# Attention of a two-layer trunk: mask by TensorE, softmax from PSUM, and the difference of two maps taken while P is turned

## The chip, the cores and the metric

The kernel runs on one core of a Trainium2 chip. The metric is the device time in microseconds (us); the median of three runs is given. The engines are TensorE (PE, and PEld for its weight loads), VectorE (DVE), ScalarE (ACT), GpSimd (POOL) and SyncE (SP), which issues the large DMAs.

## What is computed

256 tokens of width 1024 go through two layers. Layer 0 has two kinds of attention, 8 heads each: A (latent attention, query and key of 96) and B (a band with a bias by relative position, 64), then a dense SwiGLU. Layer 1 has differential attention C, 8 heads of two maps each (64), then a top-2-of-8 expert SwiGLU. All is in float32.

```python
def chunk_causal_softmax(scores, q0):          # CHUNK = 64, Q_BLOCK = 128
    mask = k_chunk[None, :] <= q_chunk[:, None]
    return softmax(where(mask, scores, -inf))
# A: for each block of 128 queries, keys up to the block's end
s = q @ k.T * scale;  p = chunk_causal_softmax(s, q0);  out = p @ v
# C: two maps m of each head
s = einsum('bhmqd,bhmkd->bhmqk', q, k) * scale
p = chunk_causal_softmax(s, q0)
a = p[:, :, 0] - lam * p[:, :, 1]
out = a @ v;  then rmsnorm(out, g_sub) * (1 - lam_init)
```

## The kernel before

Each engine has its own program, written by hand in order; semaphores join them. Weights come in units of 1 MB by SyncE's DMAs into seven buffers `raw`. ScalarE copies each unit to `w_hi` (rounded, L641 and L878), VectorE takes the rest to `w_lo` (L1027, L1430), and TensorE makes three products of each pair of blocks (L1672 to L1674). These two steps are the "split" of a unit, `split_to(n)` in both programs. A buffer is loaded again once VectorE has split its unit.

The change touches the two attention loops. Both work on units: one unit is one map, with 128 x 128 scores for the first block of queries and 128 x 256 for the second, side by side as 384 columns of one PSUM bank. Three banks (0, 1, 6) hold scores in turn.

- TensorE, layer 0 (i from 0 to 20): `scores(i)` (L1760; the products L1765 and L1766), from i = 3 `turn_p(i - 3)` (three transposes, L1779), `keep_busy(2)` (products that nobody reads, L1772), from i = 5 `weigh_values(i - 5)` (L1793 to L1795). Heads 0 to 7 are A, with 96 rows, 8 to 15 are B, with 64 rows, each in one half of the array's rows.
- TensorE, layer 1 (i from 0 to 12): the same with two units an iteration (first map on rows 0 to 63, second map on rows 64 to 127) and `keep_busy(3)`. Then `out_projection` turns y (L1807) half by half.
- VectorE, `scores` (L1128): scales a unit, adds the mask (or B's bias with the mask in it) and writes it from PSUM to SBUF (L1136), then takes the two negated maxima of each row (L1140, L1141). In layer 1 `difference(i)` runs two iterations behind: a reciprocal (L1385), a factor for each row (L1386), and p0 + factor * p1 over 384 columns in SBUF (L1390). `head_outputs` (L1302) scales the outputs, `output_norm` (L1411 to L1415) norms y. At i = 8 and 9 of layer 1 it splits units 1 and 2 of the output projection.
- ScalarE, `exponentials` (L692): two exponentials in place in SBUF with the row sums (L695, L697), then `turn_p` (L705): the turned P from PSUM to SBUF, three units behind.
- TensorE's `scores` waits until VectorE has read the bank's last unit (`scores_read`), and its `turn_p` waits for the exponential (layer 0) or for the difference (layer 1), and for the copy of the turned P of two heads before.
- GpSimd makes constants at the start (a select of 128 x 128 at L585) and issues a few small DMAs, the last (L2143) for a gain after the first unit of layer 1's output projection.

## Time and profile before

| | |
|---|---|
| median of 3 runs | 1478.47 us (1476.52 to 1480.3) |
| profiled execution | 1479.04 us, span 1476.9 us |
| busy, share of the span | PE 97%, PEld 80%, DVE 80%, ACT 65%, POOL 1% |
| chain that ended last | PE 83%, DVE 10%, ACT 3%, issue 3%, DMA 1% |
| granted PE clock | 0.991 on average |
| HBM read | 419.28 MB, 285 GB/s over the span |

A row of a timeline gives the start, the duration, engine, line, operation, output and inputs, how many instructions were merged into it, and in brackets how long the engine idled before it and what ended that. Products of TensorE overlap in their pipeline, so what one costs in a row of them is the distance from start to start. Layer 0's attention loop is at 77.5 to 118 us, layer 1's at 409.8 to 448 us, the experts from 493 us on.

### The profile page before, as it was taken

The numbers are of one execution on the slowest core, as the hardware profiler recorded it, in microseconds if no ns is written. First come the engines' busy times: TensorE is split into PE (matmuls) and PEld (weight loads), VectorE is DVE, ScalarE is ACT, GpSimd is POOL, SyncE is SP. The second block draws the span as 40 slices with busy tenths as digits, with TensorE's granted clock in tenths as the row PEclk, the third lists the DMA queues.
The fourth block names the chain that finished last, engine by engine and source line by source line (L and its number), as shares of the span: only waits on it lengthen the run. The fifth ranks groups of instructions, "written<-read, shape, count | busy, mean of one in ns | idle before, by whom it ended". The sixth has DMA issues, their size and how long they took to land.

```text
span 1476.9 us, 17986 instructions
## 1 busy us (share of the span) xinstructions
PE 1427.5 (97%) x6705; PEld 1177.5 (80%) x6705; DVE 1177.6 (80%) x1003; ACT 959.4 (65%) x835; POOL 8.4 (1%) x49
## 2 busy tenths in 40 slices
PE   7899999999979899999999999999999999999998
PEld 6778788887757788888888888878888888888886
DVE  5984545446895799899898899879888988888986
ACT  5574533344564677777777777767776776777774
POOL 2000000000000000000000000000000000000000
PEclk9999999999999899999999999999999999999999
DMA  8404755375403599999999999989999999999993
GB/s 276 155 30 154 245 183 187 115 233 173 171 27 103 189 388 364 367 368 376 335 353 379 370 347 376 377 294 366 376 365 358 372 375 309 373 377 355 369 377 113
DMA packets 181604, 421.56 MB, mean 285 GB/s; under 512 B 9240, under 2 KB 12364, under 8 KB 181516
## 3 DMA queue, kind: packets, MB, share of 16 engines
q1 hardware_dynamic: 178460, 418.56, 79.1%
q0 software_dynamic: 560, 1.59, 0.4%
q8 instruction: 58, 0.95, 0.3%
q10 hardware_dynamic: 2496, 0.23, 0.1%
q14 instruction: 30, 0.25, 0.0%
HBM read 419.28 MB, written 1.06 MB: 285 GB/s over the span
## 4 chain that ended last, share of the span: by engine, by line
PE 83%; DVE 10%; ACT 3%; issue 3%; DMA 1%; ACTq 0%; DVEq 0%
PE ps L1672 25%; PE ps L1674 25%; PE ps L1673 25%; DVE w_lo L1027 2%; PE ps L2037 2%; DVE w_lo L1430 2%; ACT w_hi L641 1%; PE ps L2003 1%; DVE h L1559 1%; DVE work L1136 1%; PE ps L1772 1%; ACT w_hi L878 1%; PE ps L1779 0%; PE ps L2015 0%; PE ps L2014 0%
## 5 line engine op out<-in xcount | busy, mean ns | idle before, releaser
L1430 DVE TENSOR_TENSOR w_lo<-raw,w_hi 128x2048 fp32r<-128x2048 f32 x336 | 768.1, 2289 | 107.9 <-ACT w_hi L878 107.2
L878 ACT ACTIVATE w_hi<-raw 128x2048 fp32r<-128x2048 f32 x336 | 644.8, 1919 | 244.7 <-PE ps L1674 244.6
L1672 PE MATMUL ps<-w_hi,xT_hi 128*128 128x512 f32 (+2 forms) x1312 | 515.6, 393 | 14.8 <-issue 4.1
L1674 PE MATMUL ps<-w_hi,xT_lo 128*128 128x512 f32 (+2 forms) x1312 | 508.5, 388 | 0.0
L1673 PE MATMUL ps<-w_lo,xT_hi 128*128 128x512 f32 (+2 forms) x1312 | 507.4, 387 | 0.0
L1672 PEld LDWEIGHTS ps<-w_hi,xT_hi 128*128 128x128 f32 x1312 | 247.3, 189 | 67.9 <-issue 8.8
L1674 PEld LDWEIGHTS ps<-w_hi,xT_lo 128*128 128x128 f32 x1312 | 247.1, 188 | 51.0
L1673 PEld LDWEIGHTS ps<-w_lo,xT_hi 128*128 128x128 f32 x1312 | 247.6, 189 | 47.3
L1672 PE MATMUL ps<-w_hi,hT_hi 128*128 128x512 f32 (+1 forms) x548 | 214.7, 392 | 2.4 <-DVE hT_lo L1041 2.4
L1027 DVE TENSOR_TENSOR w_lo<-raw,w_hi 128x2048 fp32r<-128x2048 f32 (+4 forms) x65 | 138.3, 2137 | 98.1 <-ACT w_hi L641 97.9
L1674 PE MATMUL ps<-w_hi,hT_lo 128*128 128x512 f32 (+1 forms) x548 | 213.0, 389 | 0.0
L1673 PE MATMUL ps<-w_lo,hT_hi 128*128 128x512 f32 (+1 forms) x548 | 212.9, 388 | 0.0
L641 ACT ACTIVATE w_hi<-raw 128x2048 fp32r<-128x2048 f32 (+4 forms) x65 | 115.6, 1791 | 126.2 <-PE ps L1674 126.2
L1672 PEld LDWEIGHTS ps<-w_hi,hT_hi 128*128 128x128 f32 (+1 forms) x548 | 102.9, 188 | 25.0 <-DVE hT_lo L1041 2.6
L1674 PEld LDWEIGHTS ps<-w_hi,hT_lo 128*128 128x128 f32 (+1 forms) x548 | 102.9, 188 | 21.5
L1673 PEld LDWEIGHTS ps<-w_lo,hT_hi 128*128 128x128 f32 (+1 forms) x548 | 102.9, 188 | 20.3
L905 ACT ACTIVATE hT_hi<-ps 128x512 fp32r<-128x512 f32 x56 | 33.2, 592 | 9.8 <-PE ps L2037 9.8
L1565 DVE TENSOR_TENSOR hT_lo<-ps,hT_hi 128x512 fp32r<-128x512 f32 x56 | 38.3, 683 | 1.3 <-ACT hT_hi L905 1.3
L1592 DVE TENSOR_TENSOR prod_e<-sil_e,ps 128x512 f32<-128x512 f32 x56 | 38.1, 680 | 0.0
L2037 PEld LDWEIGHTS ps<-ident,prod_e 128*128 128x128 f32 x224 | 27.1, 139 | 12.0 <-DVE h L1559 2.9
L2037 PE MATMUL ps<-ident,prod_e 128*128 128x128 f32 x224 | 33.8, 273 | 2.8 <-DVE h L1559 2.8
L930 ACT ACTIVATE sil_e<-ps 128x512 f32<-128x512 f32 x56 | 32.3, 577 | 0.0
(264 smaller groups left out, 717.0 us busy)
## 6 DMA issues: line engine op xcount, KB each, us to landing
raw<-in_od_ex_gate_dram SPq DMA_DIRECT2D x112, 1024.0 KB, 5.8
raw<-in_od_ex_up_dram SPq DMA_DIRECT2D x112, 1024.0 KB, 6.3
raw<-in_od_ex_down_dram SPq DMA_DIRECT2D x112, 1024.0 KB, 6.1
raw<-in_od_w_qkv_dram SPq DMA_DIRECT2D x12, 1024.0 KB, 5.2
raw<-in_ev_ff_gate_dram SPq DMA_DIRECT2D x10, 1024.0 KB, 5.2
raw<-in_ev_ff_up_dram SPq DMA_DIRECT2D x10, 1024.0 KB, 6.0
raw<-in_ev_ff_down_dram SPq DMA_DIRECT2D x10, 1024.0 KB, 5.0
raw<-in_ev_w_in_dram SPq DMA_DIRECT2D x5, 1024.0 KB, 8.8
```

Source lines behind the costliest of these rows:

```text
L641: ins = act.activation(w_hi[0:r, n % SPLIT, a:a + m], raw[0:r, raw_of(n), a:a + m], ACT.Copy)
L878: act.activation(w_hi[:, (DENSE + q) % SPLIT, :], raw[:, r, :], ACT.Copy).then_inc(hi_ready, 1)
L905: act.activation(hT_hi[:, :, side(m)], blocks(4 + m % 2), ACT.Copy).then_inc(hT_part, 1)
L930: act.activation(sil_e[:, j % 2, :], ps[:, 2 * (j % 2), :], ACT.Silu).then_inc(silu_done, 1)
L1027: ins = dve.tensor_tensor(w_lo[0:r, n % SPLIT, a:a + m], raw[0:r, raw_of(n), a:a + m], w_hi[0:r, n % SPLIT, a:a + m].bitcast(F32), ALU.sub ...
L1430: dve.tensor_tensor(w_lo[:, k, :], raw[:, raw_of(DENSE + q), :], w_hi[:, k, :].bitcast(F32), ALU.subtract).then_inc(lo_ready, 1)
L1565: dve.tensor_tensor(hT_lo[:, :, side(m)], blocks(4 + m % 2), hT_hi[:, :, side(m)].bitcast(F32), ALU.subtract).then_inc(hT_ready, 1)
L1592: dve.tensor_tensor(prod_e[:, j % 2, :], sil_e[:, j % 2, :], ps[:, 2 * (j % 2) + 1, :], ALU.mult).then_inc(prod_done, 1)
L1672: pe.matmul(out, x_hi, hi, start=start, stop=False)
L1673: pe.matmul(out, x_hi, lo, start=False, stop=False)
L1674: return pe.matmul(out, x_lo, hi, start=False, stop=stop)
L2037: ins = pe.transpose(ps[:, 4 + j % 2, n * P:(n + 1) * P], prod_e[:, j % 2, n * P:(n + 1) * P], ident[:, :])
```

## The change

- For units of A and C TensorE adds the mask: a third product, identity by the mask's 64 rightmost columns, over the right halves of both diagonal blocks (`scores`, argument `masked`). The factor d^-1/2 moves into the gain columns of the queries.
- VectorE then only takes maxima, from PSUM; ScalarE takes the exponentials from PSUM and writes SBUF. B is as before (`band_scores`). The score bank of a masked unit is free after its exponential.
- VectorE instead of ScalarE copies the turned P for A and C.
- In layer 1 VectorE computes the row factors only. GpSimd makes two diagonal matrices from them, and TensorE takes the difference as it turns: for each of three blocks p0^T I + p1^T diag(factor), six f32 products instead of three transposes (`turn_difference`).
- `keep_busy` is 2 instead of 3 in layer 1. VectorE splits unit 1 of the output projection at i = 4 of the loop, unit 2 after the first half of y.

The diff, without semaphore declarations and blank lines:

```diff
@@ -283,6 +283,8 @@
 pt1 = carve(work, C_MIX, 2, 384)
+diag = carve(work, 4 * C_MIX, 2 * TT, P)
@@ -689,12 +693,16 @@
-    def exponentials(u, unit, s, slot):
+    def exponentials(u, unit, s, slot, slot_head, biased):
         act.wait_ge(max_ready, unit + 1)
-        act.activation(s[:, slot, 0:P], s[:, slot, 0:P], ACT.Exp,
+        if slot_head is not None:
+            act.wait_ge(p_psum, slot_head + 1)
+        src = s[:, slot, :] if biased else ps[:, score_bank(unit % 16), :]
+        act.activation(s[:, slot, 0:P], src[:, 0:P], ACT.Exp,
                        bias=negmax[:, u, 0:1], accum_out=psum_l[:, u, 0:1])
-        act.activation(s[:, slot, P:384], s[:, slot, P:384], ACT.Exp,
+        act.activation(s[:, slot, P:384], src[:, P:384], ACT.Exp,
                        bias=negmax[:, u, 1:2], accum_out=psum_l[:, u, 1:2]).then_inc(exp_done, 1)
@@ -777,8 +785,8 @@
         if i < A_HEADS + B_HEADS:
-            exponentials(i, i, s0, i % S0)
-        if i >= TURN_LAG:
+            exponentials(i, i, s0, i % S0, i - S0 if S0 <= i < A_HEADS else None, i >= A_HEADS)
+        if i >= A_HEADS + TURN_LAG:
             turn_p(i - TURN_LAG, pt0)
@@ -855,13 +863,12 @@
             for m in range(2):
-                exponentials(2 * i + m, A_HEADS + B_HEADS + 2 * i + m, s1, (2 * i + m) % S1)
+                exponentials(2 * i + m, A_HEADS + B_HEADS + 2 * i + m, s1, (2 * i + m) % S1,
+                             16 + i - S1 // 2 if i >= S1 // 2 else None, False)
         if i == C_HEADS:
...
             square_outputs(0)
-        if i >= TURN_LAG:
-            turn_p(A_HEADS + B_HEADS + i - TURN_LAG, pt1)
     output_roots(0)
@@ -1094,6 +1101,9 @@
+        dve.tensor_scalar(gcol[:, G_AQ:G_AQ + 1], gcol[:, G_AQ:G_AQ + 1], A_QK ** -0.5, None, ALU.mult)
+        dve.tensor_scalar(gcol[:, G_CQ:G_CQ + 1], gcol[:, G_CQ:G_CQ + 1], C_DH ** -0.5, None, ALU.mult)
         dve.tensor_scalar(gcol[:, G_SUB:G_SUB + 1], gcol[:, G_SUB:G_SUB + 1], 1.0 - LAM_INIT, None,
@@ -1125,20 +1135,35 @@
-    def scores(u, unit, s, slot, factor, added, slot_head):
+    def maxima(u, src):
+        dve.tensor_reduce(negmax[:, u, 0:1], src[:, 0:P], AX.X, ALU.max, negate=True)
+        dve.tensor_reduce(negmax[:, u, 1:2], src[:, P:384], AX.X, ALU.max, negate=True).then_inc(max_ready, 1)
+    def scores(u, unit):
         dve.wait_ge(scores_psum, unit + 1)
-        if slot_head is not None:
-            dve.wait_ge(p_psum, slot_head + 1)
-        for a, n, rows in added:
-            ins = dve.scalar_tensor_tensor(out=s[:, slot, a:a + n], in0=ps[:, score_bank(unit % 16), a:a + n], scalar=factor,
+        maxima(u, ps[:, score_bank(unit % 16), :])
+    def band_scores(head):
+        u = A_HEADS + head
+        slot, row = u % S0, bias[:, head, :]
+        dve.wait_ge(scores_psum, u + 1)
+        dve.wait_ge(p_psum, u - S0 + 1)
+        for a, n, rows in ((0, P, row[:, P:T]), (P, T, row)):
+            ins = dve.scalar_tensor_tensor(out=s0[:, slot, a:a + n], in0=ps[:, score_bank(u), a:a + n], scalar=B_DH ** -0.5,
                                            in1=rows, op0=ALU.mult, op1=ALU.add)
         ins.then_inc(scores_read, 1)
-        dve.wait_ge(scores_read, unit + 1)
-        dve.tensor_reduce(negmax[:, u, 0:1], s[:, slot, 0:P], AX.X, ALU.max, negate=True)
-        dve.tensor_reduce(negmax[:, u, 1:2], s[:, slot, P:384], AX.X, ALU.max, negate=True).then_inc(max_ready, 1)
+        dve.wait_ge(scores_read, head + 1)
+        maxima(u, s0[:, slot, :])
+    def turn_p(head, pt):
+        dve.wait_ge(p_psum, head + 1)
+        if head >= 2:
+            dve.wait_ge(pv_done, head - 1)
+        dve.tensor_copy(pt[:, head % 2, :], ps[:, 2 + head % 2, 0:384]).then_inc(p_turned_vec, 1)
@@ -1309,11 +1334,11 @@
         if u < A_HEADS:
-            added, factor = [(0, 384, mask[:, :])], A_QK ** -0.5
+            scores(u, u)
         else:
-            row = bias[:, u - A_HEADS, :]
-            added, factor = [(0, P, row[:, P:T]), (P, T, row)], B_DH ** -0.5
-        scores(u, u, s0, u % S0, factor, added, u - S0 if u >= S0 else None)
+            band_scores(u - A_HEADS)
+        if TURN_LAG <= u < A_HEADS + TURN_LAG:
+            turn_p(u - TURN_LAG, pt0)
         if u in (10, 14):
@@ -1379,27 +1404,24 @@
-    def difference(i):
+    def difference_factors(i):
...
         link(dve.reciprocal(rinv[:, 2 * i:2 * i + 2, :], psum_l[:, 2 * i:2 * i + 2, :]))
-        link(dve.scalar_tensor_tensor(out=coef[:, i, :], in0=psum_l[:, 2 * i, :], scalar=lams[:, 5:6],
-                                      in1=rinv[:, 2 * i + 1, :], op0=ALU.mult, op1=ALU.mult))
-        a, b = (2 * i) % S1, (2 * i + 1) % S1
-        for t, (c0, c1) in enumerate(((0, P), (P, 384))):
-            ins = dve.scalar_tensor_tensor(out=s1[:, a, c0:c1], in0=s1[:, b, c0:c1], scalar=coef[:, i, t:t + 1],
-                                           in1=s1[:, a, c0:c1], op0=ALU.mult, op1=ALU.add)
-        ins.then_inc(diff_done, 1)
-    for i in range(C_HEADS + DIFF_LAG):
+        dve.scalar_tensor_tensor(out=coef[:, i, :], in0=psum_l[:, 2 * i, :], scalar=lams[:, 5:6],
+                                 in1=rinv[:, 2 * i + 1, :], op0=ALU.mult, op1=ALU.mult).then_inc(coef_ready, 1)
+    for i in range(C_HEADS + TURN_LAG):
         if i < C_HEADS:
             for m in range(2):
-                scores(2 * i + m, 16 + 2 * i + m, s1, (2 * i + m) % S1, C_DH ** -0.5, [(0, 384, mask[:, :])],
-                       16 + i - S1 // 2 if i >= S1 // 2 else None)
-        if i >= C_HEADS - 1:
-            split_to(AT["out1", 0, 0] + i - C_HEADS + 2)
-        if i >= DIFF_LAG:
-            difference(i - DIFF_LAG)
+                scores(2 * i + m, 16 + 2 * i + m)
+        if i == C_HEADS // 2:
+            split_to(AT["out1", 0, 0] + 2)
+        if DIFF_LAG <= i < C_HEADS + DIFF_LAG:
+            difference_factors(i - DIFF_LAG)
+        if i >= TURN_LAG:
+            turn_p(16 + i - TURN_LAG, pt1)
         if i in (7, 9):
@@ -1418,6 +1440,7 @@
     low_y(1, 0)
+    split_to(AT["out1", 0, 0] + 3)
     output_norm(1)
@@ -1757,24 +1780,57 @@
-    def scores(unit, q, k):
-        if unit % 16 >= len(SCORE_BANKS):
-            pe.wait_ge(scores_read, unit - len(SCORE_BANKS) + 1)
+    def scores(unit, q, k, masked):
+        last = unit - len(SCORE_BANKS)
+        if A_HEADS <= last < A_HEADS + B_HEADS and unit < 16:
+            pe.wait_ge(scores_read, last - A_HEADS + 1)
+        elif unit % 16 >= len(SCORE_BANKS):
+            pe.wait_ge(exp_done, last + 1)
         b = score_bank(unit % 16)
-        pe.matmul(ps[:, b, 0:P], q(0), k(P), start=True, stop=True)
-        pe.matmul(ps[:, b, P:384], q(1), k(T), start=True, stop=True).then_inc(scores_psum, 1)
+        pe.matmul(ps[:, b, 0:P], q(0), k(P), start=True, stop=not masked)
+        ins = pe.matmul(ps[:, b, P:384], q(1), k(T), start=not masked, stop=not masked)
+        if masked:
+            diagonal = ps[:, b, :].rearrange("p (t n) -> p t n", t=TT)[:, :, CHUNK:P]
+            ins = pe.matmul(diagonal, ident[:, :], mask[:, CHUNK:P].unsqueeze(1).to_broadcast([P, TT, CHUNK]),
+                            start=False, stop=True)
+        ins.then_inc(scores_psum, 1)
...
             pe.matmul(ps[:, 7, :], xT_hi[:, n, 0:P], xT_hi[:, 0:2, :].rearrange("p c n -> p (c n)"), start=True, stop=True)
+    def wait_turned(head):
+        if head < A_HEADS:
+            pe.wait_ge(p_turned_vec, head + 1)
+        elif head < A_HEADS + B_HEADS:
+            pe.wait_ge(p_turned, head - A_HEADS + 1)
+        else:
+            pe.wait_ge(p_turned_vec, head - B_HEADS + 1)
+    def turn_difference(n):
+        head, a, b = 16 + n, 2 * n % S1, (2 * n + 1) % S1
+        pe.wait_ge(diag_ready, n + 1)
+        wait_turned(head - 2)
+        for k in range(3):
+            cols_k = slice(k * P, (k + 1) * P)
+            bank = ps[:, 2 + head % 2, cols_k]
+            pe.matmul(bank, s1[:, a, cols_k], ident[:, :], start=True, stop=False)
+            ins = pe.matmul(bank, s1[:, b, cols_k], diag[:, TT * (n % 2) + min(k, 1), :], start=False, stop=True)
+        ins.then_inc(p_psum, 1)
...
         if head >= 2:
-            pe.wait_ge(p_turned, head - 1)
+            wait_turned(head - 2)
         for n in range(3):
@@ -1873,11 +1929,11 @@
         if i < A_HEADS:
-            scores(i, lambda t: qta[0:A_QK, i, t * P:(t + 1) * P], lambda n: kta[0:A_QK, i, 0:n])
+            scores(i, lambda t: qta[0:A_QK, i, t * P:(t + 1) * P], lambda n: kta[0:A_QK, i, 0:n], True)
         elif i < heads:
...
             r = slice(m * B_DH, (m + 1) * B_DH)
-            scores(i, lambda t: qtb[r, pair, t * P:(t + 1) * P], lambda n: ktb[r, pair, 0:n])
+            scores(i, lambda t: qtb[r, pair, t * P:(t + 1) * P], lambda n: ktb[r, pair, 0:n], False)
         if TURN_LAG <= i < heads + TURN_LAG:
@@ -1964,11 +2020,11 @@
                 r = slice(m * C_DH, (m + 1) * C_DH)
-                scores(16 + 2 * i + m, lambda t: qtc[r, i, t * P:(t + 1) * P], lambda n: ktc[r, i, 0:n])
+                scores(16 + 2 * i + m, lambda t: qtc[r, i, t * P:(t + 1) * P], lambda n: ktc[r, i, 0:n], True)
         if TURN_LAG <= i < C_HEADS + TURN_LAG:
             n = i - TURN_LAG
-            turn_p(16 + n, diff_done, n + 1, s1, 2 * n % S1)
-        keep_busy(3)
+            turn_difference(n)
+        keep_busy(2)
         if i >= VALUE_LAG:
@@ -2139,6 +2195,14 @@
+    for i in range(C_HEADS):
+        pool.wait_ge(coef_ready, i + 1)
+        if i >= 2:
+            pool.wait_ge(p_psum, 16 + i - 1)
+        for t in range(TT):
+            ins = pool.tensor_scalar(diag[:, TT * (i % 2) + t, :], ident[:, :], coef[:, i, t:t + 1], None, ALU.mult)
+        ins.then_inc(diag_ready, 1)
     pool.wait_ge(unit_used, AT["out1", 0, 0] + 1)
```

## Rows read from the trace of the kernel before

**Rows 1.** Busy time by stretches: each engine's busy us (instructions), PEclk, DMA share, GB/s.

```profile
77.50:130.00 52.50, 49.80 (x307) 41.92 (x308) 32.52 (x73) 31.87 (x90) 0.00 (x0) 1.00 0.07 21
...
409.50:448.00 38.50, 29.80 (x175) 21.81 (x175) 34.29 (x89) 22.79 (x77) 0.00 (x0) 0.91 0.18 55
```

**Rows 2.** Costliest groups of the page: busy us, mean ns, idle before, releaser.

```profile
L878 ACT ACTIVATE w_hi<-raw 128x2048 fp32r<-128x2048 f32 x336 | 644.8, 1919 | 244.7 <-PE ps L1674 244.6
```

**Rows 3.** Timeline of TensorE, heads of A in layer 0: start, us, [idle before <-releaser].

```profile
82.74 0.39 PE L1765 MATMUL ps<-raw 96*128 96x128 f32 x2
...
84.19 0.38 PE L1765 MATMUL ps<-raw 96*128 96x128 f32 x2
...
87.94 0.52 PE L1779 MATMUL ps<-ident,work 128*128 128x128 f32 x3 [0.74 <-ACT work L705]
```

**Rows 4.** Timeline of TensorE, one head of B in layer 0.

```profile
94.00 0.49 PE L1765 MATMUL ps<-raw 64*128 64x128 f32 x2
...
94.85 0.55 PE L1779 MATMUL ps<-ident,work 128*128 128x128 f32 x3
95.15 0.70 PE L1772 MATMUL ps<-xT_hi 128*128 128x512 f32 x2
95.70 0.33 PE L1793 MATMUL ps<-work 128*128 128x64 f32 x2
...
96.09 0.39 PE L1795 MATMUL ps<-work 128*128 128x64 f32 x2
96.40 0.48 PE L1765 MATMUL ps<-raw 64*128 64x128 f32 x2
```

**Rows 5.** Timeline of TensorE, first pair of layer 1.

```profile
409.79 0.50 PE L1765 MATMUL ps<-work 64*128 64x128 f32 x4 [0.94 <-DVE work L1126]
...
410.65 0.96 PE L1772 MATMUL ps<-xT_hi 128*128 128x512 f32 x3
```

**Rows 6.** Timeline of VectorE, layer 1's loop and its end.

```profile
429.16 0.55 DVE L1136 SCALAR_TENSOR_TENSOR work<-ps,mask 128x384 f32<-128x384 f32 x1
...
431.85 0.75 DVE L1390 SCALAR_TENSOR_TENSOR work<-work,coef 128x128 f32<-128x128 f32 x2
...
432.51 0.55 DVE L1136 SCALAR_TENSOR_TENSOR work<-ps,mask 128x384 f32<-128x384 f32 x1
...
436.46 2.28 DVE L1027 TENSOR_TENSOR w_lo<-raw,w_hi 128x2048 fp32r<-128x2048 f32 x1
...
444.92 1.22 DVE L1411 TENSOR_REDUCE ss<-work 128x8 f32<-128x1024 f32 x1 [1.12 <-ACT work L849]
```

**Rows 7.** Timeline of TensorE, layer 1's loop and its end.

```profile
429.30 0.55 PE L1779 MATMUL ps<-ident,work 128*128 128x128 f32 x3 [0.57 <-DVE work L1390]
...
430.39 0.39 PE L1793 MATMUL ps<-work 128*128 128x128 f32 x2
430.61 0.39 PE L1794 MATMUL ps<-work 128*128 128x128 f32 x2
...
439.93 0.55 PE L1779 MATMUL ps<-ident,work 128*128 128x128 f32 x3 [2.01 <-DVE work L1390]
...
448.03 1.09 PE L1807 MATMUL ps<-ident,xs 128*128 128x128 f32 x8
```

**Rows 8.** Timeline of TensorE, first products of the two output projections.

```profile
119.95 0.47 PE L1672 MATMUL ps<-w_hi,xT_hi 128*128 128x512 f32 x1 [1.62 <-issue]
...
450.95 0.47 PE L1672 MATMUL ps<-w_hi,xT_hi 128*128 128x512 f32 x1 [1.83 <-issue]
...
451.96 0.39 PE L1673 MATMUL ps<-w_lo,xT_hi 128*128 128x512 f32 x1
```

**Rows 9.** Groups of instructions of GpSimd.

```profile
L585 POOL TENSOR_SCALAR_AFFINE_SELECT ident<-ident 128x128 f32<-128x128 f32 x1 | 0.3, 282 | 0.2 <-POOL mask L583 0.2
```

**Rows 10.** Busy time by stretches, the two with the lower clock.

```profile
418.00:425.00 7.00, 6.34 (x24) 4.19 (x26) 6.25 (x20) 4.03 (x17) 0.00 (x0) 0.51 0.00 0
452.00:456.00 4.00, 4.00 (x12) 3.16 (x11) 1.61 (x3) 0.30 (x1) 0.00 (x0) 0.57 0.02 4
```

More of the change, by code:

```diff
@@ L364, in trunk @@
         exp_done = sem("exp_done")
-        diff_done = sem("diff_done")
+        coef_ready = sem("coef_ready")
+        diag_ready = sem("diag_ready")
         p_psum = sem("p_psum")
         p_turned = sem("p_turned")
+        p_turned_vec = sem("p_turned_vec")
         pv_done = sem("pv_done")
@@ L1786, in weigh_values @@
                 per = 2 if layer else 4
-                pe.wait_ge(p_turned, head + 1)
+                wait_turned(head)
                 if n % per == 0 and n >= 2 * per:
```

## The prediction

> **What bounds the kernel now.** I read the views in this order: the busy time by stretches, the timeline of TensorE (PE) and VectorE (DVE) through the two attention loops, then the clock.
>
> The stretches [rows 1] hold the two loops that the change touches. In layer 0 PE is busy 49.80 of 52.50 us at full clock: PE bounds it. In layer 1 PE is busy 29.80 of 38.50 us and DVE 34.29 of 38.50: DVE bounds it. Outside, the expert phase waits for PE alone (ScalarE's wait for a free buffer, 244.6 us in total, ends with a product [rows 2]), and its DMAs start as buffers come free, so what is won or lost in the loops passes to the end one to one.
>
> In layer 0 the timeline shows PE back to back. A head of A without values takes 84.19 - 82.74 = 1.45 us; the one stall of note is 0.74 us, for a turned P that ScalarE owes [rows 3]. A head of B takes 96.40 - 94.00 = 2.40 us: 0.85 for its scores (94.00 to 94.85), 0.30 for three transposes, 0.55 for two filler products, 0.39 up to the last value product and 0.31 from there to the next head [rows 4].
>
> In layer 1 one iteration scores a pair, two maps of 64 rows each. Where nothing holds PE, the pair takes 410.65 - 409.79 = 0.86 us [rows 5]. Two heads of 64 rows thus cost what one costs in layer 0 (0.85 [rows 4]): the two halves of the array work side by side. DVE needs 432.51 - 429.16 = 3.35 us for an iteration [rows 6], and PE idles for it: 0.57 us in the middle, 2.01 us near the end [rows 7], where two splits of 2.28 us stand in DVE's queue [rows 6]. From the first score (409.79) to the first transpose of y (448.03) it is 38.24 us [rows 5, 7].
>
> **DVE and ScalarE, part by part.** Each masked unit loses its scaled addition (0.55 us [rows 6]); the maxima stay, read from PSUM. The difference loses its two long operations (0.75 us [rows 6]) and keeps the two short ones. DVE gains the copy of P out of PSUM, 384 columns, which I take at 0.55 us, what the addition over 384 columns from PSUM takes now. An iteration of layer 1: 3.35 - 2 x 0.55 - 0.75 + 0.55 = about 2.0 us. ScalarE loses the copy. Neither is late any more, if PE's iteration gets longer than that. The two extra scalings of a gain column lie early beside products; I charge 0.1 us for them in all.
>
> **PE, layer 0.** Each of the 8 masked heads gains a product of 128x128 weights on 128 columns of f32. Its price: the start-to-start distance of two such products, 0.22 us (430.39 to 430.61 [rows 7]). 8 x 0.22 = 1.8 us. The stall of 0.74 us should go, as DVE now makes that copy and has no split before it. The banks now wait for the exponential of unit i - 3, not its reading; the turn that follows on PE waits for the same exponential anyway, so this costs little. With 0.2 us lost on that, layer 0 gets 1.2 us longer less some start-up slack: + 1.0 (bounds 0 and + 2.5, the latter if the three splits on ScalarE and DVE each show for 0.3 us and the stall stays).
>
> **PE, layer 1: the term that decides.** The mask is a product over all 128 rows, and it now stands between the scores of the first map and those of the second. They can't run side by side any more: each costs what a lone 64-row head costs in layer 0. So for one iteration:
> - scores 2 x 0.85, two masks 2 x 0.22, and 0.09 for the way back to 64 rows between them (0.31 less 0.22 [rows 4]): 2.23 us, for 0.86 before;
> - the turn: six f32 products with fresh weights, 6 x 0.22 = 1.33 us, for three transposes at 0.30;
> - fillers: two, 0.55, for three;
> - values unchanged: 0.22 + 0.22 + 0.31 = 0.75, or 0.67 where no scores follow.
>
> The loop has 3 iterations of scores and fillers (2.87 with the 0.09 back), 2 with the turn (4.20), 3 with values too (4.86), 3 with turn and values (2.55) and 2 with values (1.22): 8.6 + 8.4 + 14.6 + 7.6 + 2.4 = 41.6 us. DVE (2.0 us) and ScalarE (four exponentials, under 2 us) are far below 4.86. At the end of the loop y's first norm (3.11 us from its reduction on DVE at 444.92 to the transposes at 448.03 [rows 6, 7]) starts one copy after the last turn, while PE has 3.66 us of work after it (0.55 + 0.67 + 2 x 1.22): the two end within 0.2 us of each other, as now. So the loop goes from 38.24 to about 41.7 us: + 3.4 (bounds below, with the rivals: - 3.3 and + 6.4). Here the rule of the Trainium skill that speaks against the change is in "TensorEngine Tiling (Array Packing)", Key Properties: tiles work in parallel, but changing the tiling mode drains the engine. The trace agrees, 0.86 us for a pair against 0.85 for one. Without that rule, the pair still side by side, the sum would be that of the second rival below.
>
> **GpSimd.** It makes two diagonals of 128x128 an iteration. The nearest row is a 128x128 select at 0.28 us [rows 9]. From the last score of iteration 2 (409.8 + 7.9) DVE takes some 1.2 us for maxima and factors, so the diagonals may start at 419.0; PE wants them at 409.8 + 8.6 + 2.2 = 420.6. Up to 1.6 us for the pair is hidden at the tightest place, later over 3 us; I charge nothing (bounds 0, and 1 us if one takes four times the select). Its later DMA of a gain waits for a much later event. No DMA of the weight stream waits for GpSimd.
>
> **The moved splits.** Weight unit 1 of the output projection is split at iteration 4 on DVE, beside 4.2 us of PE; unit 2 after the first half of y. This delays the second norm by 2.2 us: now it would be ready some 3.0 us after the projection's first product, then 5.3. PE reaches the place after 24 products, four of which take 451.96 - 450.95 = 1.01 us at full clock [rows 8], so 5.5 to 6 us: just hidden (bounds 0 and 0.5). SyncE may load unit 2's buffer again only after its split, some 10 us later than now; the experts, who use it, start at 493 us, so I charge nothing.
>
> **The clock.** PE's granted clock is near 0.5 (the lower level, 1.2 GHz; 0.51 on average from 418 to 425 us, 0.57 from 452 to 456, where a part is at full speed) [rows 10], the second time after 1.83 us of idle PE [rows 8]. The first costs little now as DVE sets the pace. The second hits the projection: 4 us at 0.57 lose 1.7 us of full-speed work. In layer 0 the same end of loop, with 1.62 us idle [rows 8], has no fall. After the change the loop is dense, but the 1.83 us idle before the projection stays [rows 8]. I take half: - 0.9 (bounds 0 and - 1.7).
>
> **Sum.** 0.1 (gain columns) + 1.0 (layer 0) + 3.4 (layer 1) + 0 (GpSimd, splits) - 0.9 (clock) = + 3.6 us. The profiled execution took 1479.04 us (a span of 1476.9 and 2.1 around it), so it becomes 1482.6; the median of the three runs is 1478.47, 0.6 below the profiled one, and from it the change comes out at 1482.1 us.
>
> **The rivals.**
> - *PE keeps more overlap than I give it.* If each map costs what a head of A does, 0.60 us (1.45 less 0.30 and 0.55 [rows 3, 4]), instead of 0.85, the loop is 16 x 0.25 = 4.0 us shorter: 1478.1, no change. Against it stands each head of B in layer 0.
> - *The pair still runs side by side, mask and all.* Then scores cost 0.86 + 0.44 + 0.09 an iteration and the loop is 8 x 0.84 = 6.7 us shorter: 1475.4, faster than before, by DVE's relief. For it: nothing but that two of the three products are still of 64 rows.
> - *Slower: the lower clock comes into layer 1's loop.* PE now sets the pace there, so that a fall as at 418 us (6 us long) costs 3 us, which it doesn't today; and the fall at the projection stays, 0.9. It decides once PE idles some 2 us before the first turn, that is, if the first diagonals come 2 us late. 1486.0.
> - *The change doesn't relieve anything*: only if maxima and exponentials from PSUM were far slower than from SBUF. The 384-column addition that reads PSUM today takes 0.55 us in all [rows 6]; nothing speaks for it, and up to 4.86 us an iteration it wouldn't be seen.
>
> **Numbers.** Forecast 0.47 (own range 1479.5 to 1485), no-premium 0.15, side by side 0.12, lower clock or other stalls 0.26. 0.3% is 4.4 us, about what a measurement of this kernel tells from no change. Slower by more: a good third of the forecast's chance (above 1482.9) and nine tenths of the last, 0.40. Faster by more (below 1474.0): a third of the side-by-side case and a little: 0.06. The rest, 0.54, is within. The range 1475 to 1487.5 leaves out 2 in 10, by the loop's bounds on the one side and the stalls on the other.
>
> **What would show it.** In layer 1's loop PE busy without gaps, an iteration of scores, turn and values near 4.9 us, DVE busy for 2 us of it; the second map's first score block 0.3 us or more behind the first mask; turn products 0.22 us apart. In layer 0 the first 8 heads 0.22 us longer. Wrong, if PE waits for GpSimd, if an iteration comes out at 4 us, or if the clock in the loop is below 1.

## The result, and the profile after

The changed kernel takes 1484.97 us in the median of 20 runs (1481.88 to 1496.64), the kernel before 1478.10 (1476.43 to 1480.93), so it is 6.9 us slower by the medians (a quotient of 1.0046). The ratio on record is 1.0067, 95% interval [1.0052, 1.0082]; it is that of the means, 1488.11 and 1478.21, and so 9.9 us. The forecast was 1482.1 us, 3.6 us slower.

The 20 runs fall into two groups, and the mean granted clock of TensorE tells them apart: 13 runs at 1481.9 to 1485.9 us with a clock of 0.993 to 0.995, and 7 at 1493.5 to 1496.6 with 0.984 to 0.986. (The expectation of the first experiment below says 14 and 6, a miscount.) The kernel before has no second group. The first group is 5.8 us over before (1483.94), and the means lie further apart than the medians because of the second. The profiled execution is of the first: 1483.94 us, a span of 1482.1, which is 4.9 us more than the profiled execution of before.

| from - to | before | after | forecast |
|---|---|---|---|
| layer 0, first score to first transpose of y | 77.84 - 117.29: 39.45 | 77.90 - 118.33: 40.43 | + 1.0 |
| layer 1, the same | 409.79 - 448.03: 38.24 | 411.15 - 456.16: 45.01 | + 3.4 |
| first product of layer 1's output projection | 450.95 | 459.08 | |
| first gather of the experts | 486.91 | 493.91 | |

So layer 0 came out as forecast, and layer 1's loop got 6.8 us longer instead of 3.4. Busy time by stretches (from and to, length, then the busy us of PE, PEld, DVE, ACT, POOL, then PEclk, DMA share, GB/s), to be set beside [rows 1] and, for the last, [rows 10]:

```profile
410.00:415.00 5.00, 4.06 (x21) 2.40 (x19) 2.12 (x6) 3.27 (x9) 0.00 (x0) 1.00 0.00 0
415.00:420.00 5.00, 5.00 (x25) 3.16 (x24) 2.11 (x8) 3.01 (x14) 0.00 (x0) 1.00 0.00 0
...
435.00:440.00 5.00, 5.00 (x33) 4.02 (x32) 2.10 (x7) 1.82 (x8) 1.18 (x2) 1.00 0.00 0
...
460.00:465.00 5.00, 5.00 (x17) 3.95 (x17) 3.74 (x4) 0.30 (x1) 0.00 (x0) 0.71 0.54 166
```

PE is full and DVE at 2.1 of 5 us, where DVE stood at 34.29 of 38.50 [rows 1]: the bound moved to PE. One iteration with scores, turn and values on PE's timeline (start us, us; a row of x2 is one f32 product):

```profile
434.26 0.48 PE L1793 MATMUL ps<-work 64*128 64x128 f32 x2
434.59 0.59 PE L1794 MATMUL ps<-work 64*128 64x256 f32 x2
435.11 0.49 PE L1798 MATMUL ps<-mask,ident 128*128 128x128 f32 x2
435.53 0.48 PE L1793 MATMUL ps<-work 64*128 64x128 f32 x2
435.86 0.59 PE L1794 MATMUL ps<-work 64*128 64x256 f32 x2
436.38 0.49 PE L1798 MATMUL ps<-mask,ident 128*128 128x128 f32 x2
436.70 0.39 PE L1826 MATMUL ps<-ident,work 128*128 128x128 f32 x2
436.93 0.39 PE L1827 MATMUL ps<-work 128*128 128x128 f32 x2
...
437.96 0.71 PE L1806 MATMUL ps<-xT_hi 128*128 128x512 f32 x2
438.51 0.38 PE L1849 MATMUL ps<-work 128*128 128x128 f32 x2
...
439.27 0.49 PE L1793 MATMUL ps<-work 64*128 64x128 f32 x2
```

The two maps stand one behind the other (L1798 is the mask); the pair of [rows 5], where both lay in one row of x4 and took 0.86 us, is gone. The iteration takes 439.27 - 434.26 = 5.01 us. From a map's mask to the next map's score it is 0.42 us (435.11 to 435.53), from the second mask to the turn 0.32 (436.38 to 436.70), where two products of 128 rows stand 0.22 to 0.23 apart.

The idle times of PE in the loop and behind it:

```profile
447.28 0.49 PE L1826 MATMUL ps<-ident,work 128*128 128x128 f32 x2 [0.34 <-POOL work L2203]
456.16 1.09 PE L1863 MATMUL ps<-ident,xs 128*128 128x128 f32 x8 [1.41 <-DVE xs L1437]
459.08 0.47 PE L1695 MATMUL ps<-w_hi,xT_hi 128*128 128x512 f32 x1 [1.83 <-issue]
```

One more wait for GpSimd, of 0.19 us, stands at 431.60. A wait costs more than the idle time in brackets, since the products behind it start late as well. By the starts, the first of these turns comes 0.36 us late (0.68 us after its mask for 0.32) and loses 0.09 more inside; the second comes 0.50 us late (0.73 us after the last value product, 0.23 at 449.85). Together they cost 0.95 us. GpSimd's diagonals, by its groups of instructions:

```profile
L2203 POOL TENSOR_SCALAR work<-ident,coef 128x128 f32<-128x128 f32 x16 | 9.5, 602 | 414.5 <-DVE coef L1412 414.5
```

And DVE at the loop's end, where the 1.41 us come from:

```profile
450.12 0.56 DVE L1166 COPY work<-ps 128x384 f32<-128x384 f32 x1 [2.17 <-PE ps L1851]
450.59 0.68 DVE L1327 TENSOR_TENSOR xs<-ps,rinv 128x512 f32<-128x512 f32 x1
452.59 0.56 DVE L1166 COPY work<-ps 128x384 f32<-128x384 f32 x1 [1.32 <-PE ps L1851]
453.06 1.21 DVE L1433 TENSOR_REDUCE ss<-work 128x8 f32<-128x1024 f32 x1
454.64 0.20 DVE L1435 RECIPROCAL rs<-rs 128x8 f32<-128x8 f32 x1 [0.37 <-ACT rs L861]
454.88 1.22 DVE L1437 TENSOR_TENSOR xs<-xs,rs 128x1024 f32<-128x1024 f32 x1
```

DVE is idle 2.17 and 1.32 us in front of its last two copies. Each copy waits for the values of the head two before (L1851), which must have read the buffer of pt1 that the copy overwrites, and the norm of the first half of y (L1433 to L1437) is queued behind the copies. It ends at 456.10; PE has had no work since 454.75.

### The profile page after: what moved, and what is told of

Its sections match the earlier page's. It is cut to its first block, busy times and chain, and to the rows that moved or that the text cites. A ratio compares the mean times of both kernels' runs of the same rounds, so it can differ in the third digit from the quotient of the medians.

```text
span 1482.1 us, 18184 instructions
## 1 busy us (share of the span) xinstructions
PE 1441.3 (97%) x6812; PEld 1190.4 (80%) x6812; DVE 1168.0 (79%) x981; ACT 951.3 (64%) x819; POOL 17.9 (1%) x65
## 4 chain that ended last, share of the span: by engine, by line
PE 84%; DVE 9%; ACT 3%; issue 3%; DMA 1%; POOL 0%; ACTq 0%; DVEq 0%; POOLq 0%
PE ps L1695 25%; PE ps L1697 25%; PE ps L1696 25%; DVE w_lo L1034 2%; PE ps L2093 2%; DVE w_lo L1453 1%; PE ps L2059 1%; ACT w_hi L645 1%; DVE h L1582 1%; PE ps L1806 1%; PE ps L1794 1%; PE ps L1793 1%; ACT w_hi L885 1%; PE ps L1798 0%; PE ps L2071 0%
## 5 line engine op out<-in xcount | busy, mean ns | idle before, releaser
L1615 DVE TENSOR_TENSOR prod_e<-sil_e,ps 128x512 f32<-128x512 f32 x56 | 38.1, 680 | 0.0
```

The source lines that it names most:

```text
L1615: dve.tensor_tensor(prod_e[:, j % 2, :], sil_e[:, j % 2, :], ps[:, 2 * (j % 2) + 1, :], ALU.mult).then_inc(prod_done, 1)
```

## The experiments

All comparisons are against the kernel before, run beside them (medians 1477.36, 1477.88 and 1478.62 us for the three sets of runs). The ratio need not be the quotient of the medians; it lies above it where some runs are of the second group. "Loop" is layer 1's, from the first score to the first transpose of y, in the profiled execution.

| kernel | us (median) | ratio, interval | loop us | runs with a clock of 0.987 or less |
|---|---|---|---|---|
| as changed | 1484.53 | 1.0052 [1.0033, 1.007] | 45.01 | 9 of 28 |
| masks_after_pair | 1481.28 | 1.0023 [1.0014, 1.0031] | 42.83 | 0 of 11 |
| copy_on_scalar | 1480.34 | 1.0028 [1.0011, 1.0045] | 43.05 | 1 of 11 |
| no_fillers_l1 | 1481.51 | 1.0041 [1.0024, 1.0058] | 40.91 | 3 of 12 |
| turn_one_map | 1478.92 | 1.001 [1.0, 1.002] | 39.35 | 1 of 11 |
| fillers_before_loop | 1483.92 | 1.0041 [1.0028, 1.0055] | 45.02 | 0 of 5 |
| the same again | 1484.64 | 1.0047 [1.0035, 1.006] | 45.02 | 0 of 6 |
| pair_and_copy | 1477.33 | 0.9997 [0.9986, 1.0007] | 38.25 | 0 of 11 |
| layer0_alone | 1476.94 | 0.9996 [0.9987, 1.0005] | 37.64 | 0 of 11 |
| pair_copy_one_filler | 1479.24 | 1.0009 [0.9998, 1.0019] | 36.90 | 0 of 12 |
| pair_copy_no_filler | 1477.80 | 0.9998 [0.999, 1.0007] | 38.96 | 0 of 12 |
| one_filler_both_layers | 1472.26 | 0.9957 [0.9944, 0.997] | 36.90 | 0 of 5 |

(The first row has the time of the experiment, the loop of the first profile and the runs of both. The medians take in the runs with the low clock. Without them they are 1483.94 us as changed, 1480.2 for copy_on_scalar, 1481.05 for no_fillers_l1 and 1478.8 for turn_one_map. The low run of turn_one_map is further off than the others, 1500.89 us at a clock of 0.977; it was not profiled. Of the kernel before, none of 101 runs is more than 3.3 us above the median of its set; one, of 1481.12 us, has a clock of 0.987.)

### The changed kernel once more: the second group of times

> The changed kernel itself, nothing left out. 6 of its 20 runs took 1493 to 1497 us at a mean granted clock near 0.985, the other 14 took 1482 to 1486 at 0.993 to 0.995. Theory C (the clock falls in layer 1's attention loop, where TensorE now sets the pace, and stays low over much of it): about 3 runs in 10 lie 10 to 13 us above the rest with a clock near 0.985. Rival (the fall lies in another stretch, which the kernel before has too): the kernel before shows such runs as often in the same rounds.

Two of its 8 runs were at 1494.7 and 1495.0 us with a clock of 0.985, and the profiled execution (a span of 1493.2) is one of them. So this trace shows what the second group is. PE at the loop's head:

```profile
412.40 0.46 PE L1793 MATMUL ps<-work 64*128 64x128 f32 x2 [0.94 <-DVE work L1136]
412.69 0.59 PE L1794 MATMUL ps<-work 64*128 64x256 f32 x2
...
416.06 0.79 PE L1793 MATMUL ps<-work 64*128 64x128 f32 x2
416.65 1.06 PE L1794 MATMUL ps<-work 64*128 64x256 f32 x2
...
421.51 0.79 PE L1793 MATMUL ps<-work 64*128 64x128 f32 x2
```

and by stretches:

```profile
415.00:420.00 5.00, 5.00 (x15) 2.82 (x13) 1.25 (x4) 2.10 (x10) 0.00 (x0) 0.50 0.00 0
...
430.00:435.00 5.00, 5.00 (x20) 3.70 (x18) 1.48 (x5) 1.82 (x8) 1.18 (x2) 0.50 0.00 0
435.00:440.00 5.00, 5.00 (x31) 3.69 (x30) 3.00 (x5) 1.83 (x8) 0.00 (x0) 1.00 0.00 0
```

The clock falls to its lower level (0.50, 1.2 GHz) at 414.5 us and stays there for 20 us, though PE is busy all the time. An iteration of scores and fillers takes 421.51 - 416.06 = 5.45 us; in the first profile it takes 3.00. Twenty us of full PE at half clock are 10 us of work lost, and the medians of the groups lie 11.2 us apart. In the two profiles (spans of 1482.1 and 1493.2) 9.3 of 11.1 us are in the loop, 54.28 for 45.01; another 1.25 us were lost ahead of it, with a clock of 0.98 for 1.00 from 118 to 200 us. Before, the same stretch has its fall too [rows 10], but DVE sets the pace there and it costs little (0.6 us, by layer0_alone below).

### Both scores, then both masks

```diff
 # layer 1, TensorE
 for m in range(2):
     scores(16 + 2 * i + m, ..., True)     # without its mask product
+for m in range(2):
+    add_mask(16 + 2 * i + m)              # the mask product, then scores_psum
```

> In layer 1 the scores of both maps are issued first, the two mask products after them. Nothing is left out. Theory A (the mask between the two maps ends their running side by side and adds two switches of the array's row mode an iteration): the pair costs 0.9 us again, an iteration of scores, turn and values falls from 5.0 to about 3.8 us, and the kernel is 8 x 1.2 = 9 to 10 us faster than the changed one, near 1475. Rival B (the number of products sets the loop, not their order): no change, 1484 to 1485.

Measured: 1481.28 us, 3.2 less than the changed kernel (2.7 less than its first group) where 9 to 10 were expected, and the loop 2.2 us shorter. The pair is in one row again:

```profile
435.11 0.50 PE L1793 MATMUL ps<-work 64*128 64x128 f32 x4
435.43 0.61 PE L1794 MATMUL ps<-work 64*128 64x256 f32 x4
435.97 0.71 PE L1807 MATMUL ps<-mask,ident 128*128 128x128 f32 x4
436.52 0.39 PE L1834 MATMUL ps<-ident,work 128*128 128x128 f32 x2
...
439.08 0.50 PE L1793 MATMUL ps<-work 64*128 64x128 f32 x4
```

The pair takes 435.97 - 435.11 = 0.86 us, the very figure of [rows 5], and the iteration 439.08 - 435.11 = 3.97 us instead of 5.01. So one product of 128 rows between two 64-row maps is enough to end their running side by side. A wait for a bank isn't what did it: in iteration 0 all banks are free, and there too the maps start 1.24 us apart as changed and together here. The loop didn't get 8 x 1.04 us shorter, since other waits came up. In iterations 1 to 3 the second map starts 1.04 us behind the first, and the iterations take 3.00, 3.00 and 4.33 us as before this edit. By the program its bank is free only after the exponential of three units before; the idle time that ScalarE ends there shows in pair_copy_one_filler. And one turn waits long for GpSimd:

```profile
430.82 0.77 PE L1834 MATMUL ps<-ident,work 128*128 128x128 f32 x2 [1.53 <-POOL work L2213]
```

The factors of that head stand on DVE behind the split of iteration 4, 2.28 us long. The clock fell in that place too (0.66 from 430 to 435 us). This iteration takes 7.39 us (427.72 to 435.11) for 5.46 as changed, so it gives back 1.9 of the 4 us that the whole pairs gain. The 1.41 us at the loop's end stayed.

### The turned P copied by ScalarE again

```diff
-# VectorE, layer 1:   if i >= TURN_LAG: turn_p(16 + i - TURN_LAG, pt1)
+# ScalarE, layer 1:   if i >= TURN_LAG: turn_p(A_HEADS + B_HEADS + i - TURN_LAG, pt1)
```

> In layer 1 ScalarE copies the turned P again, as before the change; all else as changed. Theory D (TensorE's 1.41 us of idle at the loop's end and its short waits for GpSimd come from VectorE, which stands in its copy until the values of two heads before are done, with the factors and the norm queued behind): the idle goes, the loop ends 1.5 to 2 us earlier, 1482.5 to 1483.5 us. Rival (the norm's chain is late whoever copies): no change.

Measured: 1480.34 us, 4.2 less than the changed kernel (3.7 between the first groups); the loop 43.05 us. In front of the transposes of y the idle time is gone, for DVE gets to its reduction early:

```profile
448.39 0.69 DVE L1329 TENSOR_TENSOR xs<-ps,rinv 128x512 f32<-128x512 f32 x1 [2.66 <-PE ps L1851]
450.20 1.22 DVE L1433 TENSOR_REDUCE ss<-work 128x8 f32<-128x1024 f32 x1 [1.12 <-ACT work L857]
...
454.33 1.23 DVE L1437 TENSOR_TENSOR xs<-xs,rs 128x1024 f32<-128x1024 f32 x1
```

It now reduces at 450.20, before the last two copies are due, and the scaling ends at 455.56, when PE's own work ends too (455.55). The queue behind the copies on VectorE was the cause of the 1.41 us. But the copies hold up the norm on ScalarE as well. Its root of the sum of squares (L861) stands behind the last copy, and DVE waits 2.68 us for it:

```profile
453.39 0.49 ACT L713 ACTIVATE work<-ps 128x384 f32<-128x384 f32 x1 [1.98 <-PE ps L1851]
453.77 0.29 ACT L861 ACTIVATE rs<-ss,eps 128x8 f32<-128x8 f32 x1
454.10 0.20 DVE L1435 RECIPROCAL rs<-rs 128x8 f32<-128x8 f32 x1 [2.68 <-ACT rs L861]
```

Only the root, the reciprocal and the scaling are left behind the last copy there, where on VectorE the reduction stands behind it too, and what is left just hides under PE's own work. The loop is 2.0 us shorter, 1.3 from there and 0.5 from the second wait for GpSimd, which went as well. The median gives 2 us more than the loop; the traces don't show from where (the profiled execution, 1484.05 us, is itself the slowest of the ten without the low clock). The one run at 1493.72 us is of the second group.

### No fillers in layer 1's loop

```diff
-                keep_busy(2)        # layer 1
+                keep_busy(0)
```

> The changed kernel without any filler product in layer 1's loop. Theory E (TensorE sets the pace, the fillers cost their full time and the clock holds without them): 13 x 0.5 us = 6 us faster, near 1479, clock as before. Rival C (the fillers hold the clock up in a loop of short f32 products): more of the runs, or all, lie 10 us higher or more, with a clock of 0.985 or below.

Measured: 1481.51 us and a loop of 40.91, 4.1 less, with PE idle for 2.02 us at its end. The two fillers are worth 0.46 to 0.50 us an iteration by the starts (three iterations of scores took 2.50, 2.54 and 2.53 us for 3.00), 6 us in all. Two thirds of that came through; the rest went into longer waits, of PE for GpSimd (0.65, 0.32 and 0.34 us) and at the end. So PE sets the pace of most of the loop but not of all of it, and theory E's 6 us were too many. 3 of 12 runs were at 1490.1 to 1491.5 us with a clock of 0.987: the second group needs no fillers, and the fillers don't keep it off.

### The turn of one map alone

```diff
-pe.matmul(bank, s1[:, a, cols_k], ident[:, :], start=True, stop=False)
-ins = pe.matmul(bank, s1[:, b, cols_k], diag[...], start=False, stop=True)
+ins = pe.transpose(bank, s1[:, a, cols_k], ident[:, :])
```

> The changed kernel, layer 1 turning only the first map's P by three transposes; the second map and its diagonals are left out of the turn (they are still made). Theory (layer 1's loop is bound by TensorE, so each product counts): 24 products of 0.22 us go, 5.3 us, and the waits for GpSimd, 0.5 us: 1484.5 - 5.8 = 1478.7 us. Rival (the loop is bound by the chain of copies and values, pt's two buffers): under 2 us gained, 1482.5 us or more.

Measured: 1478.92 us, 5.6 less than the changed kernel; the loop 39.35, 5.7 less. That is what was expected, 5.8, but the agreement is luck. The edit also puts a transpose in place of each first product, and a transpose costs less:

```profile
436.07 0.49 PE L1826 MATMUL ps<-ident,work 128*128 128x128 f32 x3
436.31 0.71 PE L1806 MATMUL ps<-xT_hi 128*128 128x512 f32 x2
```

Three transposes take 0.24 us here (436.07 to 436.31) where the six products take 1.26 (436.70 to 437.96 in the first profile). An iteration without a wait is 1.02 us shorter (3.99 for 5.01), 8 us over eight heads and not 5.3. Some 2.5 us of that go back into waits for GpSimd, since PE comes earlier (1.20, 0.87, 0.38 and 0.28 us idle), and the end still has its 1.42. What the experiment shows is that the loop is bound by PE's products, against the rival's 2 us. The turn's price in the forecast is shown by the rows of the changed kernel, 0.22 us from one product to the next.

### Fillers in the idle time ahead of the loop

```diff
+for n in range(5): pe.matmul(ps[:, 4, :], xT_hi[:, n, 0:P], ...)   # 128x512, unread
 pe.wait_ge(qk_normed, 3)
 ...
+for n in range(3): pe.matmul(ps[:, 4, :], xT_hi[:, n, 0:P], ...)
 pe.wait_ge(proj_vec[1], QKV_J)
```

> The changed kernel with 5 and 3 unread products of 128x512 in TensorE's two idle times before layer 1's loop (1.43 and 0.94 us). Theory (the clock falls at the head of the loop in some runs because of the idle time before it): no run with a mean clock near 0.985 and 10 us more; the others as the changed kernel, 1483.8 us. Rival (the fall comes from the loop's own short products): about 3 in 10 runs are at 1493 to 1497 us as before.

> The same kernel as fillers_before_loop, for more executions of it: five were too few to tell a share of 3 in 10 from none. Theory (the idle time before the loop lets the clock fall): again no run with a mean clock near 0.985, all at 1483 to 1486 us. Rival (the loop's own short products do it): about 3 in 10 at 1493 to 1497 us.

(Two waits for the bank, in front of the five, are left out of this cut.) PE's idle times of 1.45 and 0.94 us became 0.31 and 0.24. All 11 runs have a clock of 0.992 to 0.995 and 1483.2 to 1487.2 us; the rest of the loop is as it was, 45.02 us. With a share of 9 in 28 for the changed kernel, eleven in a row without one happen by chance (19/28)^11 = 1.4 times in 100. So the idle time ahead of the loop very likely has a part in it. It isn't all. Four kernels have their masks behind both maps and that same idle time (masks_after_pair, pair_and_copy, pair_copy_one_filler, pair_copy_no_filler), and 0 of their 46 runs have a mean clock of 0.987 or less; four have the mask between the maps and the idle time (as changed, copy_on_scalar, no_fillers_l1, turn_one_map), with 14 of 62. So the runs speak for both together as what the 20 us fall needs. That it is the pairs isn't shown: in iterations 1 to 3, where the long fall runs, the maps stand apart with the masks behind them too, and one of these four, pair_copy_no_filler, has a fall of 10 us in just that place (below), short enough for its mean clock to stay at 0.991. How the chip weighs all this stays open.

### The edits together, and layer 0 by itself

pair_and_copy joins the first two edits and moves the split away from the factors:

```diff
-                if i == C_HEADS // 2:
+                if i == 9:
                     split_to(AT["out1", 0, 0] + 2)
```

> The changed kernel with three edits to layer 1 at once: both maps' scores before both masks, the turned P copied by ScalarE again, and VectorE's split of a weight moved from iteration 4 (where the factors of a head stood behind it) to iteration 9. Theory (the loss is made of separate terms: broken pairs, copies that wait ahead of the norm, factors that wait behind the split): the gains of the first two add up, 1484.5 - 3.2 - 4.2 = 1477.1 us, and the waits of TensorE for GpSimd and for the norm at the loop's end are gone; the loop lasts 42.8 - 1.5 - 1.4 = 39.9 us. Rival (one cover for the other: what one edit frees, the next wait takes): no better than the better of the two, 1480.3 us.

Measured: 1477.33 us, ratio 0.9997. That is 0.2 us from the 1477.1 worked out, and the loop is 38.25 us, that of before. No idle time stands at its end; two waits for GpSimd are left, 0.16 and 0.22 us. The agreement in the time doesn't prove the sum, for it had no term for the split and the loop is 1.65 us shorter than the 39.9 expected. The split's place is the reason: iteration 5 takes 3.97 us (428.03 to 432.00) for the 7.39 in masks_after_pair, 3.4 us less, of which the expectation counted the idle 1.5 and not the clock's fall behind it. With that 42.83 - 3.4 - 1.3 = 38.1 us, near the 38.25. So each of the three edits has its term in the loop.

layer0_alone gives layer 1 its code of before (the scaling of C's gain column goes as well) and keeps layer 0 as changed.

> The changed kernel with layer 1 as it was before (mask and difference on VectorE, three fillers, copies by ScalarE, splits where they were); layer 0 and the gain columns as changed. Theory (layer 0's masks cost 1.0 us on TensorE and nothing comes back): 1477.4 + 1.0 = 1478.4 us, the loop of layer 1 38.2 us long again, no run with a mean clock near 0.985. Rival (layer 0's later end shifts what follows, and the rest of the loss is there): over 1480 us.

Measured: 1476.94 us, ratio 0.9996 [0.9987, 1.0005], so the 1.0 us of layer 0 can't be told from nothing in the time. In its trace it is there: 79.07 to 119.50 is 40.43 us, as in each kernel with this layer 0 and two fillers, against 39.45 before. Layer 1's loop was 37.64 us, 0.6 shorter than before, as the clock didn't fall in it (1.00 from 410 to 450 us). None of its 11 runs has a clock of 0.991 or less; of the 27 runs of before beside them 11 have. Among runs at 0.993 and above the medians are 1476.9 and 1476.6. Why the old loop keeps its clock behind the new layer 0 isn't settled.

Then fewer fillers, on top of pair_and_copy.

```diff
-                keep_busy(2)        # layer 1
+                keep_busy(1)        # pair_copy_one_filler; (0): pair_copy_no_filler
-                keep_busy(2)        # layer 0
+                keep_busy(1)        # one_filler_both_layers, with (1) in layer 1
```

> pair_and_copy with one unread product of 128x512 instead of two in each iteration of layer 1's loop. Theory (TensorE sets the pace of that loop): 13 products of 0.27 us less, 3.5 us, but the last five iterations wait for the copies (0.5 us): the loop 38.25 - 3 = 35.2 us, the time 1477.3 - 3 = 1474.3 us. Rival (the copies' chain with pt's two buffers takes the pace over at once): a gain of at most 1 us, 1476.3 us or more.

> pair_and_copy without the unread products in layer 1's loop. Theory: 26 products of 0.27 us less is 7 us of TensorE's time, of which some 4.1 us came back in no_fillers_l1 (loop 45.0 to 40.9 us): the loop about 34.2 us, 1473.3 us, and clock falls at its end and at the projection in some runs (up to 1 us given back). Rival (the clock falls inside the loop in most runs): 1478 us or more.

> pair_and_copy with one unread product instead of two in each iteration of both layers' loops. Theory (layer 0's loop is bound by TensorE, 49.8 us busy of 52.5): 21 products of 0.27 us less in layer 0, 5.7 us, of which VectorE's and ScalarE's chains let 3 us through; with layer 1's 3 us: 1471.3 us. Rival (layer 0's band heads are paced by ScalarE and VectorE, 1.6 us a head): nothing more than pair_copy_one_filler gains, 1474.3 us.

With one filler the loop is 36.90 us, 1.35 shorter and not 3, as PE now waits for ScalarE's exponentials in the first iterations (three times 0.35 us), for GpSimd (0.39 and 0.45) and for the norm (0.51). The time isn't shorter at all (1.0009): it is within the rival's bound, but the rival's reason, a chain that takes over at once, isn't what the loop shows. From the first gather of the experts to the end the profiled run takes 993.0 us (484.99 to 1478.0), pair_and_copy 989.5, before 990.0, after 988.2 and layer0_alone 986.1. This last stretch is the same code in all of them and differs by up to 7 us between these executions; it can hide what 1 or 2 us in a loop do; whether it did here is open. Without fillers the time, 1477.80 us, is near the rival's 1478. 10 of the 12 runs have a clock of 0.992 or less, of pair_and_copy's 11 one. In the profile the clock falls inside the loop, from about 415 to 425 us:

```profile
417.00:422.00 5.00, 5.00 (x16) 3.48 (x16) 1.45 (x6) 2.25 (x11) 1.19 (x2) 0.50 0.00 0
422.00:427.00 5.00, 5.00 (x27) 4.16 (x26) 1.46 (x6) 2.21 (x9) 1.18 (x2) 0.63 0.02 3
```

and the loop is 38.96 us, longer than with one. So in these profiles one filler is worth its time to the loop and the second isn't; the medians tell neither (1479.24 with one, 1477.33 with two). With one filler in both layers the time is 1472.26 us, 6.4 less than before (0.9957, five runs) and 7.0 less than with one in layer 1 alone; 21 x 0.27 = 5.7 us of unread products left layer 0. No trace shows that gain whole. The profiled execution is the slowest of the five (1476.36), and its layer 0 takes 41.41 us, longer than the 40.43 with two fillers: it is 2.0 us ahead by 106.7 us, where PE has been idle for 1.15, and then the clock falls (0.50 from 107 to 115). The other four, 1470.9 to 1472.5, would be without the fall, but that is argued and not seen. This version beats both kernels. Its gain owes nothing to the change, as far as the runs go: fewer fillers in layer 0 of the kernel before weren't tried.

## Why the prediction was off

- **What bounds.** Right. PE bounded layer 0 and DVE layer 1; after, PE bounds both but for the waits below. That a loss passes to the end one to one can't be told to the microsecond: of 7.0 us at the first gather the profiled runs show 5.2 at the end of the span, and the expert stretch between moves by more than that by itself.
- **Layer 0, + 1.0.** Right to the tenth in the trace: 40.43 for 39.45 us. A head of A without values takes 1.67 for 1.45, and the stall of 0.74 [rows 3] is gone. DVE's copy takes 0.56 us for the 0.55 I took.
- **The pair broken by its mask.** Right as a mechanism. The rivals "side by side, mask and all" and "more overlap" (0.60 us a map) are dead: with the mask between, a map's scores cost 0.85 us (435.11 - 434.26); with both masks behind, the pair 0.86. Here the Trainium skill, "TensorEngine Tiling (Array Packing)", Key Properties, says that tiles work in parallel and that a change of the tiling mode drains the engine, and the trace agrees. The size was somewhat off: I gave a mask 0.22 us and the way back to 64 rows 0.09 once an iteration. Measured, it is 0.42 from the first mask to the second map and 0.32 from the second mask to the turn, 0.3 us an iteration more than twice 0.22, of which 0.09 were in the sum. The iterations of scores and fillers took 3.00 for 2.87, those with the turn 4.34 for 4.20, and one with all and no wait 5.01 for 4.86. Over eight iterations that is 1.0 of the 3.3 us missing (45.01 - 41.7).
- **GpSimd, 0.** A diagonal took 0.60 us and not 0.28, so twice the nearest row; the pair of them 1.2. Two waits of PE, 0.19 and 0.34 us idle and 0.95 by the starts, at the edge of my bounds of 0 and 1. What I had not seen is that the factors stand behind the split of iteration 4 in DVE's queue (the first wait), and later behind a copy that waits for values (the second, gone in copy_on_scalar). masks_after_pair shows the split's price once PE is quicker: 1.53 us idle, 3.4 with the clock's fall behind it.
- **The moved splits behind the loop, 0.** Right: from its first product to the turn of h (L1708, L1685 before) the output projection takes 23.00 us, before 23.03.
- **The end of the loop: the step that failed.** I let y's norm begin "one copy after the last turn" and end within 0.2 us of PE's work. But there are two buffers of turned P, so the copies of the last heads wait for the values of two heads before, and the values come with fillers in between. The last copy ran at 452.59, 1.5 us after PE's last turn had ended (451.11), and the outputs (L1327), the squares and the reduction, each behind it or behind the copy before, were late. From the reduction (453.06) to the transposes (456.16) it is 3.10 us, as I took it; the start was wrong, and it cost 1.41 us of idle PE. Before the change ScalarE had this wait in its queue, with the root of the norm behind it but not the reduction. copy_on_scalar shows it: same products, no idle time.
- **The clock, - 0.9.** Wrong in its place. The fall at the projection is there as before (0.71 from 460 to 465 us), as the 1.83 us of idle PE are. Of the other eleven profiles with the changed layer 1, or a version of it, three are without it, and there the projection takes 21.4 us and not 23.0, so the fall costs 1.6 us, near the 1.7 that I had as its bound. What came back instead I hadn't looked at: from the first product of the router to the next product behind it (L2040 to L2045, L1984 to L1989 before) it takes 6.30 us for 7.40, at a clock of 0.89 for 0.66. All twelve of these profiles have 6.3 to 6.4 us there, before and layer0_alone 7.4. So near - 0.9 is luck. Why the router's clock gains isn't known.
- **The slower rival.** I gave the lower clock in layer 1's loop 0.26 and a price of 3 us for 6 us of it. It came in 9 of 28 runs, at about 11 us each, and lasted 20 us in the one profiled. Its trigger wasn't late diagonals: the fall began before the first turn. The sum has nothing for it, and in the means it is the largest part of what is missing: 7 of 20 runs at 11 us are 4 of the 9.9 us. So this is the second step that failed.
- **The sum.** 1.0 and 3.4 as forecast, + 1.0 (mode changes), + 1.0 (GpSimd) and + 1.4 (the norm behind the copies) give 7.8 us by the first product of the projection (459.08 - 450.95 = 8.1 measured); the router gives 1.1 back, 7.0 at the first gather. No row shows the 0.1 us for the gain columns. The runs of the first group (19 of 28, with a clock of 0.993 or more) have a median of 1483.94, 5.8 over before; the second group brings the median of the 20 to 6.9 and the mean to 9.9.

## What to carry to other kernels

Before a step is moved to a queue, ask what its waits will hold up there: the copy was the same half microsecond on both engines, but on VectorE the reduction of the norm stood behind it. Work out when the last such step can start from what it waits for, not from the product before it. Where two narrow products run side by side, anything of full height goes behind both and not between them: that order alone was worth 2.2 us of the loop and about 3 of the time. And when PE becomes the bound of a stage, a fall of its clock that used to be nearly free is paid in full, so look where the trace of before already has one, and take enough runs to see whether the times fall into groups.

## What the runs showed of the hardware

- Two 64-row f32 maps of 128 and 256 columns take 0.86 us side by side, and one alone takes 0.85. From a mask (128 rows) to a map (64 rows) it is 0.42 us, from a mask to the turn (both 128 rows) 0.32, between two f32 products of the turn 0.22. Three f32 transposes of the same blocks take 0.24 to 0.30 together.
- The granted clock stayed at 0.50 for 20 us under a PE that was busy without a gap, with scores of 64 rows, masks and fillers; it came back at 435 us, after the first turn. (The one trace shows it; that the other runs with a low mean clock are the same is read from that clock.) Kernels with the mask between the maps had a mean clock of 0.987 or less in 14 of 62 runs, those with the masks behind both in none of 46, and there was none in 11 where the idle times of 1.4 and 0.9 us ahead were filled.
- GpSimd scales a 128x128 f32 tile by a column in 0.60 us; a select over the same tile takes 0.28 [rows 9].
- VectorE's maxima over 128 and 256 columns cost the same from PSUM as from SBUF within 0.01 us, 0.29 and 0.41 us.
